# Norms whose sums of squares are split over four column groups, and weights whose first unit is loaded one stage earlier

## The reference

```python
def _rms_norm(x, g):                       # block 1: attn_norm, ffn_norm, and per head q and k norms
    y = xf * lax.rsqrt(jnp.mean(xf * xf, axis=-1, keepdims=True) + EPS)
    return (y * g)

def layer_norm(x, g, b):                   # block 2: conv_ln, ln2
    mu = jnp.mean(xf, -1, keepdims=True); var = jnp.mean(jnp.square(xf - mu), -1, keepdims=True)
    return (xf - mu) * lax.rsqrt(var + EPS_2) * g + b

def l2_normalize(x):                       # block 2: q and k of the delta rule
    return xf * lax.rsqrt(jnp.sum(jnp.square(xf), -1, keepdims=True) + 1e-6)

# block 3: h = modulate(rmsnorm(x, attn_norm_w), sa, sca); ctx likewise; q and kv latents; per head diff norm
#          x = x + gf * moe(modulate(rmsnorm(x, ffn_norm_w), sf, scf)); return rmsnorm(x, final_norm_w)
# every block: projections h @ w before and after attention-like mixers, then a feed-forward or expert part
```

## Time and profile before

| | us |
|---|---|
| median of 3 runs | 4125.99 (4120.43 to 4131.15) |
| the profiled execution | 4129.73 |
| its span in the profile | 4127.9 |
| TensorE busy | 3511.0 (85%) |
| VectorE busy | 2328.0 (56%) |
| ScalarE busy | 1536.9 (37%) |
| GpSimd busy | 140.4 (3%) |

### The profile page before, as it was taken

One profiled execution on the slowest core, in us unless ns is written; L12 is line 12 of the kernel. 1 busy time (PEld: TensorE's weight loads), 2 busy tenths in 40 slices (PEclk: granted clock), 3 DMA queues, 4 the chain that ended last, 5 costly groups with the idle time before them and its releaser, 6 DMA issues. The chain is left out here.

```text
span 4127.9 us, 45959 instructions
## 1 busy us (share of the span) xinstructions
PE 3511.0 (85%) x15671; PEld 2637.0 (64%) x15672; DVE 2328.0 (56%) x2916; ACT 1536.9 (37%) x1926; POOL 140.4 (3%) x124
## 2 busy tenths in 40 slices
PE   6778798999958688899879778775999999999996
PEld 4646687774446457688652645554777777777774
DVE  3355675338232245445440547435888888888885
ACT  1143332010023431110110215314777777777772
POOL 0000000000000100000000000002000000000001
PEclk8889999999979899699989889977999999999997
DMA  4311222222111100022216300116999999999995
GB/s 144 104 47 42 82 91 93 77 95 82 62 36 46 32 11 1 27 95 99 81 61 232 102 31 19 34 58 273 387 361 366 353 362 365 355 350 363 363 351 197
DMA packets 172315, 653.53 MB, mean 158 GB/s; under 512 B 14953, under 2 KB 82377, under 8 KB 114226
## 3 DMA queue, kind: packets, MB, share of 16 engines
q1 hardware_dynamic: 154370, 605.44, 40.2%
q0 software_dynamic: 7568, 25.70, 1.7%
q10 hardware_dynamic: 10272, 20.98, 1.3%
HBM read 610.98 MB, written 36.77 MB: 157 GB/s over the span
## 5 line engine op out<-in xcount | busy, mean ns | idle before, releaser
L378 DVE TENSOR_TENSOR experts_rest<-experts_weights,experts_leading 128x2048 fp32r<-128x2048 f32 x384 | 875.3, 2286 | 100.1 <-ACT experts_leading L2894 100.1
L2894 ACT CAST experts_leading<-experts_weights 128x2048 fp32r<-128x2048 f32 x384 | 715.4, 1904 | 46.9 <-ACT experts_y L2886 23.1
L384 PE MATMUL psum<-experts_leading,experts_xT_leading 128*128 128x512 f32 x1024 | 409.3, 400 | 51.6 <-DVE experts_rest L378 51.6
L385 PE MATMUL psum<-experts_rest,experts_xT_leading 128*128 128x512 f32 x1024 | 406.8, 397 | 0.0
L386 PE MATMUL psum<-experts_leading,experts_xT_rest 128*128 128x512 f32 x1024 | 402.5, 393 | 0.0
L384 PEld LDWEIGHTS psum<-experts_leading,experts_xT_leading 128*128 128x128 f32 x1024 | 194.6, 190 | 107.8 <-DVE experts_rest L378 65.4
L386 PEld LDWEIGHTS psum<-experts_leading,experts_xT_rest 128*128 128x128 f32 x1024 | 194.4, 190 | 44.6
L385 PEld LDWEIGHTS psum<-experts_rest,experts_xT_leading 128*128 128x128 f32 x1024 | 194.9, 190 | 40.2
L384 PE MATMUL psum<-experts_leading,experts_hidden_leading 128*128 128x512 f32 x512 | 210.3, 411 | 0.0
L386 PE MATMUL psum<-experts_leading,experts_hidden_rest 128*128 128x512 f32 x512 | 202.0, 394 | 0.0
L385 PE MATMUL psum<-experts_rest,experts_hidden_leading 128*128 128x512 f32 x512 | 200.9, 392 | 0.0
(11 more groups left out here) (664 smaller groups left out, 6923.2 us busy)
## 6 DMA issues: line engine op xcount, KB each, us to landing
experts_weights<-in_w_up SPq DMA_DIRECT2D x256, 1024.0 KB, 6.9
experts_weights<-in_w_down SPq DMA_DIRECT2D x128, 1024.0 KB, 6.8
merge_weights<-in_w_merge SPq DMA_DIRECT2D x32, 768.0 KB, 4.2
ada_weights<-in_w_ada SPq DMA_DIRECT2D x24, 1024.0 KB, 6.8
ff_up_weights<-in_w_up SPq DMA_DIRECT2D x22, 1024.0 KB, 4.8
expert_rows<-experts_y ACTq DMA_DIRECT2D x66, 256.0 KB, 7.2
down_weights<-in_w_down SPq DMA_DIRECT2D x16, 704.0 KB, 5.1
out_weights<-in_w_out SPq DMA_DIRECT2D x6, 1536.0 KB, 8.7
```

What stands on the lines that cost most here:

```text
L378: return dve.tensor_tensor(out, src, leading.bitcast(F32), ALU.subtract)
L384: pe.matmul(out, lh, rh, start=start, stop=False)
L385: pe.matmul(out, lh, rl, start=False, stop=False)
L2894: act.copy(leading[h % LEADING], place(ring, h)).then_inc(masked, 1)
```

## The change

Both kinds of norm sum per token quarter: four matmuls per chunk, each with 32 columns of stationary data and 128 tokens, write to partitions 0-31, 32-63, 64-95 and 96-127 of one bank. Root and reciprocal run on 128 x 128 (128 partitions, 128 tokens of the quarter). Four matmuls with 32 rows each spread the quarters over 128 partitions into four banks, and the last multiplication reads the four banks in one operation. Squares are made by ScalarE (even chunks) and VectorE (odd chunks), the ring has four buffers, and ScalarE makes a square root of one number at the start of the stage, which loads the table there. In nsa_norm the short chunk `cmp_flat` comes fifth instead of last.

The first weight unit of twelve stages (proj1, out1, ff_up, proj2a, proj2b, proj2c, merge, out2, ple, proj3, proj3b, out3) has a place of its own at the top of the memory and semaphores of its own, and is loaded in the stage before (or in the one during which its place is free): `FirstUnit` and the `then=` arguments. VectorE splits this unit before the source, and TensorE waits for source chunks one by one. `ple_in` and `ctx_in` go; their loads are issued in out2 and ln2. The eight skewed copies are issued in attn_norm. `combine` gathers into 16 buffers, and its load of the residual waits for gather 6. Clearing of `zeros` moves to a rotation stage.

```diff
+        "striped": np.arange(STRIPE)[None, :] == row % STRIPE,
...
+def striped(ap):
+    return ap.rearrange("p (j c) -> p j c", j=STRIPES)
...
-def feature_norm(k, name, groups, matrix, scale, eps, shift=None, memory=()):
+def feature_norm(k, name, groups, scale, eps, shift=None, memory=(), then=None):
...
+            @block.gpsimd
+            def _(pool):
+                pool.tensor_copy(first_rows[:, :], k.c("striped")[:, 0:1].broadcast_to([P, P])).then_inc(picked, 1)
...
+                act.activation(warm[:, :], k.c("one"), ACT.Sqrt).then_inc(warmed, 1)
+                for i, (g, _, s) in enumerate(flat):
+                    if i % 2 == 0:
+                        if i >= 4:
+                            act.wait_ge(summed, i - 3)
+                        act.activation(sq[:, i % 4, 0:width[g]], s, ACT.Square).then_inc(squared[0], 1)
+                for g in range(len(groups)):
+                    act.wait_ge(summed, until[g])
+                    act.activation(std[:, g, 0:part[g]], k.bank(g, part[g]), ACT.Sqrt, bias=k.c(eps), scale=scale
+                                   ).then_inc(rooted, 1)
...
-                    pe.matmul(k.bank(g % 2, width[g]), matrix, sq[:, n % 3, 0:width[g]], start=(s == 0),
-                              stop=(s == len(groups[g][0]) - 1)).then_inc(summed, 1)
+                for i, (g, n, _) in enumerate(flat):
+                    pe.wait_ge(squared[i % 2], i // 2 + 1)
+                    for j in range(STRIPES):
+                        last = pe.matmul(k.psum[j * STRIPE:(j + 1) * STRIPE, g * BANK:g * BANK + part[g]], k.c("ones")[:, 0:STRIPE],
+                                         sq[:, i % 4, j * part[g]:(j + 1) * part[g]], start=(n == 0),
+                                         stop=(n == len(groups[g][0]) - 1))
+                    last.then_inc(summed, 1)
...
+                    for j in range(STRIPES):
+                        rows = slice(j * STRIPE, (j + 1) * STRIPE)
+                        last = pe.matmul(k.bank(4 + j, part[g]), first_rows[rows, :], rstd[rows, g, 0:part[g]], start=True, stop=True)
+                    last.then_inc(spread, 1)
...
+                for i, (g, _, s) in enumerate(flat):
+                    if i % 2:
+                        if i >= 4:
+                            dve.wait_ge(summed, i - 3)
+                        dve.tensor_tensor(sq[:, i % 4, 0:width[g]], s, s, ALU.mult).then_inc(squared[1], 1)
...
-                    dve.reciprocal(r, std[:, g % 2, 0:width[g]]).then_inc(turned, 1)
+                    dve.reciprocal(rstd[:, g, 0:part[g]], std[:, g, 0:part[g]]).then_inc(turned, 1)
+                    dve.wait_ge(spread, g + 1)
+                    r = striped(k.psum[:, 4 * BANK:8 * BANK])[:, :, 0:part[g]]
...
+                            dve.scalar_tensor_tensor(striped(out[n]), striped(s), gain[n], r, ALU.mult, ALU.mult).then_inc(scaled, 1)
...
 chunk_norms
-                    if n >= 4:
-                        pe.wait_ge(scaled, n - 3)
-                    pe.matmul(k.bank(1 + n % 4, width[n]), column[:, n * P:(n + 1) * P], rstd[:, 0:width[n]], start=True, stop=True).then_inc(spread, 1)
+                    if n >= 2:
+                        pe.wait_ge(scaled, n - 1)
+                    for j, lo, hi in stripes(n):
+                        here = slice(j * STRIPE, (j + 1) * STRIPE)
+                        last = pe.matmul(k.bank(4 * (n % 2) + j, hi - lo), column[here, n * P:(n + 1) * P], rstd[here, 0:hi - lo],
+                                         start=True, stop=True)
+                    last.then_inc(spread, 1)
...
+class FirstUnit:
+    def __init__(self, k, name, pieces, size, below=0):
+        self.slot = k.high(f"{name}_first", [P, size], below)
...
+    def load(self, sp, sem):
+        for (place, src), landed in zip(self.pieces, self.landed):
+            sp.dma_start(place, src).then_inc(landed, 16)
...
 project
+        ring = [first.slot if first and i == 0 else sb(f"weights{i}", [P, size]) for i in range(2)]
...
+                        if first and q == 0 and isinstance(u, int) and u == 0:
+                            return
...
-                                if j == 0 and s.split and source_chunks and kk in (0, half):
-                                    pe.wait_ge(source_split, source_chunks - s.kc + (s.kc if kk else half))
+                                opens = isinstance(u, int) and u == 0
+                                if j == 0 and s.split and source_chunks and (kk == 0 or opens):
+                                    pe.wait_ge(source_split, source_chunks - s.kc + (kk + 1 if opens else s.kc))
...
+                if first:
+                    split_unit(0, 0, starts[0] % 2, 0, only=0)
                 split_source(range(own // 2))
-                split_unit(0, 0, starts[0] % 2, 0, only=0)
+                if not first:
+                    split_unit(0, 0, starts[0] % 2, 0, only=0)
                 split_source(range(own // 2, own))
...
+    def ple_loads(sp, sem):
+        landed = sem("p_landed")
+        sp.dma_start(per_layer[:, :, :], k.dram["pT"].rearrange("(c p) t -> p c t", p=P)).then_inc(landed, 16)
+        w_ple.load(sp, sem)
+        sp.wait_ge(landed, 16)
...
 combine
+                sp.wait_ge(gathered[N // 2 - 2], 16)
                 sp.dma_start(k.x[:, :, :].rearrange("p k t -> p (k t)"), residual).then_inc(back, 16)
...
-                    if n >= 4:
-                        pool.wait_ge(weighed, n - 3)
-                    pool.indirect_dma_start(out=got[:, n % 4, :], out_offset=None, in_=results,
+                    pool.indirect_dma_start(out=got[:, n, :], out_offset=None, in_=results,
```

More of the change, by code:

```diff
@@ L1288, in feed_forward_up @@
     with k.stage("ff_up") as (sb, sem):
[L1289 removed]
+        ring = [first.slot, sb("weights1", [P, width])]
         leading = sb("leading", [P, 2, width], F32R)
[L1291 removed]
+        rest = [k.over(f"ff_up_rest{i}", x[:, :], [P, width]) for i, x in enumerate(ring)]
         source = Parts(sb("source_leading", [P, KD, T], F32R), k.over("ff_up_source_rest", src[:, :, :], [P, KD, T]))
@@ L1387, in _, with first_block, loads @@
                 pairs(dve, body)
-def first_block(k, skewed, lines_skewed):
+def first_block(k, lines, skewed, lines_skewed):
     with ExitStack() as ctx:
-        first_norm(k, k.x, k.h, "attn_norm", "attn_norm")
+        w_q = first_unit(k, "proj1", Section(k.dram["w_in_q"], 1, KD, None, None, None))
+        def loads(sp, sem):
+            w_q.load(sp, sem)
+            for h in range(NSA_HEADS):
+                sp.dma_start(skewed[h].rearrange("(p w) -> p w", w=SKEW + 1)[:, 0:SKEW],
+                             lines[h:h + 1, :].broadcast_to([P, SKEW])).then_inc(lines_skewed, 16)
+        first_norm(k, k.x, k.h, "attn_norm", "attn_norm", then=loads)
         with ExitStack() as mixers:
@@ L1482, in _, with gated_products @@
                     dve.scalar_tensor_tensor(s, k.bank(0), -1.0 / (n * P), s, ALU.mult, ALU.add).then_inc(centered, 1)
-def gated_products(k, name, weights, loops, kc_gate, source_gate, bias, kc, source, base, out):
+def gated_products(k, name, weights, loops, kc_gate, source_gate, bias, kc, source, base, out, first, then=None):
     nc, N = k.nc, KD
@@ L2327, in second_projections @@
                     width=2 * GDN_HEADS + 8, by_tokens=True),
-        ], beside=convolutions(k, Raw(), wide, acc, short))
+        ], beside=convolutions(k, Raw(), wide, acc, short), first=w_z)
         rates(k, rate, g, beta, log_f)
@@ L2333, in second_projections @@
         feature_center(k, "conv_center", chunks)
-        feature_norm(k, "conv_ln", [(chunks, chunks, [k.p("conv_ln_g", n) for n in range(4)])], k.c("ones"), 1.0 / 512,
-                     "eps_2")
+        w_qc = first_unit(k, "proj2c", Section(d["w2_q_c"], 2, KD, None, None, None, chunks=2))
+        feature_norm(k, "conv_ln", [(chunks, chunks, [k.p("conv_ln_g", n) for n in range(4)])], 1.0 / 512,
+                     "eps_2", then=w_qc.load)
         activate(k, "conv_silu", ACT.Silu, [(acc[:, n, :], acc[:, n, :], k.p("conv_ln_b", n)) for n in range(4)])
@@ L2524, in mixers @@
         paired_attention(k, "diff", pairs, lambda at_: mix[:, at_[0], at_[1] * P:(at_[1] + 1) * P], joined=True)
-        chunk_norms(k, "diff_norm", [(mix[:, n, :], mix[:, n, :], subln[:, :]) for n in range(DIFF_HEADS)], 1, 1.0 / P, "eps")
+        w_uq = first_unit(k, "proj3b", Section(d["w3_uq"][0:1], 1, 2, None, None, None, chunks=3))
+        chunk_norms(k, "diff_norm", [(mix[:, n, :], mix[:, n, :], subln[:, :]) for n in range(DIFF_HEADS)], 1, 1.0 / P, "eps",
+                    then=w_uq.load)
         scale = (P + DH) ** -0.5
```

384 lines of the change are left out of this document (217 added, 167 removed).

## The result

| | us |
|---|---|
| before, median of 4 runs | 4127.32 |
| after, median of 4 runs | 4015.50 (4008.15 to 4017.38) |
| ratio | 0.9725, 95% interval 0.9709 to 0.9742 |
| after, the profiled execution | 4017.08 (span 4015.3) |

The kernel is faster by 111.8 us. The forecast was 3980 (146 us) with a range of 3950 to 4030, which holds the time; its own range, 3955 to 4005, doesn't. By the total alone rival C (4013) or B (4024) would fit better than the forecast; only the stages tell them apart. So 35 us of the expected gain are missing, and the experiments are about them.

A forecast was written before the change was run, and what follows sets the result against it. Outside TensorE-bound stretches, one engine works while others wait. Norms 93.9, heads 13.5 + 19.6, removed stages 10.7, copies 4.6, combine 6.0, less 2, give 146.3 us off 4126.0: 3980; own range 3955 to 4005, 8 in 10 3950 to 4030.

The forecast's parts named there:

- rival C: Stage heads: early weights bring little because VectorE's chain sets the start; nothing of 33.1 us remains, 4013; chance 0.10.
- rival B: Norm sums: four column groups don't overlap beyond two, or not at all, and sums pace the norm; 4024; chance 0.13.
- Squares and sums: First steps of a norm: squares 3.5 us on ScalarE, 3.9 on VectorE; only the last chunk's sums show, ending at 4.6.
- Four column groups: Norm sums, four matmuls a chunk: they overlap, 0.3 us a chunk at full clock, up to 0.65 at half.
- spreading: New norm step between reciprocal and multiplication: 0.9 us, bounds 0.4 to 1.15, with TensorE at half clock.
- Multiplications: Last norm step, reading PSUM: no change from SBUF, 5.4 us for eight chunks.
- rival E: Norm multiplications: a VectorE read across four PSUM banks stalls at each, 175 us more, 4155; chance 0.02.
- Heads: Starts of twelve stages, with early first weight units: 13.5 us less in six, 19.6 together in the others.
- Rival D: TensorE's idle gaps before stages shrink to about 3 us and the clock doesn't fall; 3960; chance 0.08.
- Stages gone: Removing ctx_in (5.8 us) and ple_in (4.9 us), whose loads were waited for: 10.7 us less.
- combine: Gathers without buffer waits: 36.3 us becomes 30 at 410 GB/s, 6.0 less; bounds 0 and 11.
- Cold clock: Cost at the delta rule, which now starts with TensorE at half clock: 2 us.

The follow-up runs named there:

- aligned: The kernel after with every tile at a multiple of 64 bytes, its new constants staying where the change put them: 4004.81 us, ratio 0.9695.
- table_later: The kernel aligned with ScalarE's one-column root, which brings the table load, behind its squares instead of ahead in both norm functions: 3985.22 us, ratio 0.9651.
- norms_only: The kernel before with the new norms and their constants alone: 4071.85 us, ratio 0.9856.
- after_const_high: The kernel after with the three changed or added constants at the far end of memory and the early weight units 480 bytes lower: 4006.57 us, ratio 0.9695.
- moved_256: after_const_high with 64 unused columns (256 bytes) ahead of the other tiles: 4000.09 us.
- before_aligned: The kernel before with every tile at a multiple of 64 bytes: 4126.04 us, ratio 0.9989.
- moved_32: after_const_high with 8 unused columns (32 bytes) ahead of the other tiles: first execution 10870.16 us, run again 4017.40 us.

## Why the prediction was right or wrong

The direction and the order of size held, and so did the mechanism of every edit. That the time lies in the range is in part luck: the range held it because it reached past rival B, and half of what was missing came from something that stood in no rival. Point by point:

- **Squares and sums** (4.6; measured 5.14 in ffn_norm, with the first multiplication at 7.57 and the end at 12.93 for 12.2). The working counted 3.5 for ScalarE behind its table load and 3.9 for VectorE, but then left TensorE only the last chunk. Behind late squares the last four chunks come in a heap, and TensorE, at half clock by then, takes 0.42 each (eight matmuls from 390.64 to 391.06). The sums in the kernel after, then in aligned, where the same instructions happened to find full clock (third column from the end):

```profile
389.46:392.57 3.11, 3.10 (x64) 2.08 (x64) 1.29 (x2) 1.62 (x3) 0.00 (x0) 0.68 0.66 274
392.28:394.76 2.48, 2.47 (x64) 1.38 (x64) 1.29 (x2) 1.62 (x3) 0.00 (x0) 1.00 0.84 347
```

In aligned they end 4.5 after the start and the norm at 12.0, as forecast. So in ffn_norm the miss is the clock, not the table load, which the forecast had; table_later shows that moving the load is worth more than the miss. All 14 norms came out 0.4 to 1.0 above their forecasts, at mean clocks of 0.50 to 0.81, and gained 83.7 for 93.9; for the others the cause wasn't separated.
- **Four column groups** overlap: 64 matmuls of 128 columns take 3.11 us, where rival B had 8 times 0.6 to 1.09 at full clock and double at half. B is dead.
- **Root 0.37, reciprocal 0.95, spreading 1.01** answer to 0.36, 0.9 and 0.9. **Multiplications** from PSUM take 5.35 for eight, with 5.39 from SBUF before: reading across four banks costs nothing, rival E is dead, and the 5.6 us that the Trainium skill's figures ("VectorE: DVE Perf Modes", section on the TRN2 errata) would add don't exist here.
- **Heads**: 33.1 forecast, 35.5 by the difference to norms_only. Rival C is dead. In ff_up the 4.8 came (first product 9.1 to 4.3) and TensorE's busy time took 3.8 back (244.4, then 248.2).
- **Rival D** (the clock doesn't fall) holds in places only: proj1 and ff_up start at 0.50, out1's head has 1.00.
- **Stages gone**: ctx_in 5.7 (5.8). Inputs with attn_norm gave 14.2 (13.9).
- **combine**: 3.1 for 6.0. The gathers are issued without waits, as forecast, but the 410 GB/s that I took from one full window isn't the mean. Over the 28.8 us behind the first gather's issue, the start in them, it is 347 (last column), and 0.6 of the 10.6 MB land outside them:

```profile
3959.06:3987.90 28.84, 20.54 (x52) 11.57 (x53) 14.54 (x13) 0.00 (x0) 17.79 (x16) 0.62 0.94 347
```
- **Cold clock**: 3.9 for 2 at the delta rule, and much the same in all eight kernels with the new norms as the change has them (138.8 to 139.3; 137.5 in table_later). Token rows lose 2.3, not foreseen. mla attention's 3.2 comes and goes with the granted clock and is no cost of the change: 80.8 at 0.98 in after_const_high and 84.1 at 0.94 in moved_256, with the same instructions, and 84.1 at 0.94 in before_aligned as well.
- **Missing altogether**: where the tiles lie. "In the expert stage ... the change doesn't touch it" is the sentence that failed. It cost 13.9 there and some 3.8 in ff_up, half of the 35.

Norms 10.2, experts 13.9, ff_up 3.8, combine 2.9, delta rule 1.9, mla 3.2 and token rows 2.3 make 38.2; heads and a few stages that were better than forecast give some 4 back.

## What to carry to other kernels

Longer constants move all that lies behind them: look at where the tiles start, modulo 64 first, before and after a change, and time the untouched stages first. When one engine's work is shortened, ask again where its table load stands: what was under cover may now be the head of the chain. Price what TensorE has to catch up on at the slower clock. And a transfer-bound stage is priced by its mean rate, with the ramp, not by its best window.

## What the runs showed of the hardware that was not expected

- Tiles 32 bytes past a multiple of 64 made TensorE's passes of 128x512 slower, by the median from 388 to 398 ns in the passes by the sources' rest, and the expert stage longer by some 13 us: five kernels with its sources, hidden values and results there took 1235.6 to 1236.9, the eight others 1221.1 to 1226.0 (one profiled execution each). How it comes about (the operand itself, or what other engines write meanwhile) is open. In ff_up a multiple of 64 was no cure (TensorE busy for 248.4 us in aligned, 244.1 in after_const_high).
- One execution, moved_32's first, took 10870 us, with a granted clock of 1.00 throughout. First its passes by the sources' rest in the expert stage (busy us, mean ns), then those of the same kernel later:

```profile
L462 PE MATMUL psum<-experts_leading,experts_xT_rest 128*128 128x512 f32 x1024 | 866.5, 846 | 0.0
```
```profile
L462 PE MATMUL psum<-experts_leading,experts_xT_rest 128*128 128x512 f32 x1024 | 411.1, 401 | 0.0
```

VectorE's splitting took 2286 and 2285 ns in the two. What held TensorE back isn't in the profile; the granted clock doesn't tell it.
- The table load of 1.28 us is followed by the next activation at once (in table_later at 391.67, behind 390.38 + 1.28).
